# One wide matmul for the two parts of an operand, with a weight load and the first turn of a loop moved beside it

## What is computed

```python
h = rms_norm(x, g_mix)
q, k, v, cb, cc, cx, ga, gc = jnp.split(h @ w_in + b_in, pts, axis=-1)
q, k = apply_rope(q, positions), apply_rope(k, positions)
y_attn = sliding_window_attention(q, k, v, sinks) @ w_attn_o
y_conv = (cb * causal_short_conv(cc * cx, w_conv)) @ w_conv_o
merged = jax.nn.sigmoid(ga) * y_attn + jax.nn.sigmoid(gc) * y_conv
x = x + merged @ w_out
h = rms_norm(x, g_ffn)
x = x + moe_ffn(h, w_router, b_router, w_gate, b_gate, w_up, b_up, w_down, b_down)
return rms_norm(x, g_final)
```

## Time and profile before

| | us |
|---|---|
| median of 3 executions | 1192.78 |
| lowest, highest | 1192.71, 1193.74 |
| the profiled execution, its own time | 1192.05 |
| its span in the trace | 1190.2 |

### The profile page before, as it was taken

How to read it: one execution, slowest core, us unless ns; L and a number is a source line. 1 busy time by engine, 2 the same in 40 slices (tenths; PEclk the granted TensorE clock), 3 DMA queues, 4 the chain that set the end, 5 groups by cost and what they waited for, 6 DMA issues and landing times.

```text
span 1190.2 us, 18119 instructions
## 1 busy us (share of the span) xinstructions
PE 1119.3 (94%) x7454; PEld 572.4 (48%) x7454; DVE 364.4 (31%) x653; ACT 212.5 (18%) x393; POOL 128.2 (11%) x98
## 2 busy tenths in 40 slices
PE   8899999999999999999999999999999999999996
PEld 7899999984343333333333333333333333333342
DVE  6966785673111122111111111111111111111121
ACT  5566655451000000000000000000000000000001
POOL 4453444430000000000000000000000000000000
PEclk9999999999999999999999999999999999999999
DMA  8444666799999999999999999999999999999995
GB/s 283 143 154 157 220 201 217 245 399 413 427 428 426 428 428 428 428 428 428 428 428 428 428 428 427 428 426 428 428 428 428 430 428 428 429 429 428 427 426 218
DMA packets 71834, 448.06 MB, mean 376 GB/s; under 512 B 5497, under 2 KB 45781, under 8 KB 46709
## 3 DMA queue, kind: packets, MB, share of 16 engines
q1 hardware_dynamic: 71328, 446.75, 91.2%
q10 hardware_dynamic: 469, 0.77, 0.2%
HBM read 446.06 MB, written 1.05 MB: 376 GB/s over the span
## 4 chain that ended last, share of the span: by engine, by line
PE 48%; DMA 45%; DVE 3%; issue 2%; ACT 1%; SPq 0%; DVEq 0%; ACTq 0%
PE psum L686 26%; DMA ring<-in_w_up 23%; DMA ring<-in_w_gate 17%; PE psum L465 9%; PE psum L469 4%; DMA ring<-in_w_down 3%; PE psum L699 2%; PE psum L651 2%; DMA ring<-in_w_out 1%; PE psum L712 1%; DMA ring<-in_w_in 1%; ACT work L1016 1%; DVE w L1107 1%; PE psum L666 1%; PE psum L482 0%
## 5 line engine op out<-in xcount | busy, mean ns | idle before, releaser
L686 PE MATMUL psum<-ring,work 128*64 128x512 f32 x3072 | 686.3, 595 | 50.7 <-DMA ring<-in_w_gate 28.9
L686 PEld LDWEIGHTS psum<-ring,work 128*64 128x64 f32 x3072 | 212.4, 137 | 473.8 <-issue 363.1
L1343 DVE TENSOR_SCALAR work<-psum 128x512 f32<-128x512 f32 x32 | 22.1, 692 | 417.4 <-PE psum L686 417.4
L1476 POOL TENSOR_TENSOR w<-ring,w 128x1024 fp32r<-128x1024 f32 x38 | 100.7, 2657 | 108.0 <-ACT w L873 105.5
L1514 POOL COPY chosen<-pick 96x64 bf16 (+1 forms) x32 | 7.5, 234 | 868.8 <-PE psum L712 868.8
L465 PE MATMUL psum<-hL,w 128*128 128x256 f32 x384 | 95.3, 286 | 1.1 <-ACT w L873 0.6
L465 PE MATMUL psum<-hH,w 128*128 128x256 f32 x384 | 94.1, 283 | 0.0
L1107 DVE TENSOR_TENSOR w<-ring,w 128x1024 fp32r<-128x1024 f32 x38 | 80.1, 2112 | 37.7 <-ACT w L873 37.7
L1348 DVE TENSOR_SCALAR work<-psum 128x512 f32<-128x512 f32 x32 | 22.1, 692 | 192.8 <-PE psum L686 192.8
L873 ACT CAST w<-ring 128x1024 fp32r<-128x1024 f32 x74 | 74.4, 1048 | 27.8 <-PE psum L469 20.2
L465 PEld LDWEIGHTS psum<-hL,w 128*128 128x128 f32 x384 | 73.6, 192 | 4.0 <-issue 2.2
(11 more groups left out here) (202 smaller groups left out, 833.4 us busy)
## 6 DMA issues: line engine op xcount, KB each, us to landing
ring<-in_w_gate SPq DMA_DIRECT2D x64, 2048.0 KB, 38.1
ring<-in_w_up SPq DMA_DIRECT2D x63, 2048.0 KB, 39.7
ring<-in_w_down SPq DMA_DIRECT2D x61, 2048.0 KB, 39.3
ring<-in_w_in SPq DMA_DIRECT2D x26, 1024.0 KB, 5.0
ring<-in_w_down SPq DMA_DIRECT2D x6, 1024.0 KB, 37.6
ring<-in_w_conv_o SPq DMA_DIRECT2D x4, 1024.0 KB, 5.0
ring<-in_w_attn_o SPq DMA_DIRECT2D x4, 1024.0 KB, 5.2
ring<-in_w_out SPq DMA_DIRECT2D x4, 1024.0 KB, 6.2
```

What stands on the lines that cost most here:

```text
L686: mm = pe.matmul(psum[64 * h:64 * h + 64, b, :], src[:, k, :], w[:, k2, h * 512:(h + 1) * 512], start=(bias_of is None and k == 0), stop=( ...
L1343: v.tensor_scalar(gm, psum[:, 4, :], LIMIT, None, ALU.min).then_inc(gmin_ready, 1)
L1476: g.tensor_tensor(wL[:, par, 0, :, :], slot(s).rearrange("p (k n) -> p k n", k=KB)[:, :, 0:P], wH[:, par, 0, :, :].bitcast(F32), ALU.subtr ...
```

## The change

- Seven of the eight output-projection pieces go through a new function, `project_both`: zH and zL (and aH and aL) now lie side by side in one tensor, and one matmul with 512 columns multiplies wH with both. The high sum and the low sum land in two halves of a bank; each half m has a bank of its own, so pieces use pairs of banks. ScalarE copies the low sums to SBUF (`low_taken`), VectorE adds them to the high sums before it multiplies with the gate. The last a piece stays as it was.
- ScalarE's order in this stage: the split of the next piece before the cast of mH of the pair before.
- SyncE: the load into z's slot stands before the third `w_out` piece, the load into a's slot alone before the fourth.
- First turn: ScalarE's split of piece 3 stands ahead of the loop and of the copies of k; in the loop, `split_high_in_turn(i, 1)` at the start of a turn becomes `split_high_in_turn(i, 7)` at the end of the turn before it.
- One unused matmul before the ranks in place of two.

```diff
+PAIRS = ((4, 5), (0, 1), (2, 3))
...
-        zH, zL = parts("zH", at_slot(6), [P, KB, T]), parts("zL", at_slot(7), [P, KB, T])
-        aH, aL = parts("aH", at_slot(8), [P, KB, T]), parts("aL", at_slot(9), [P, KB, T])
+        zz, aa = parts("zz", at_slot(6), [P, 2, KB, T]), parts("aa", at_slot(8), [P, 2, KB, T])
+        zH, zL, aH, aL = zz[:, 0], zz[:, 1], aa[:, 0], aa[:, 1]
...
             for nth, src in enumerate(tail):
-                if n == NP1 - 1:
+                if n == NP1 - 2:
                     sp.wait_ge(blocks_done, 2 * (NIN + 2 * NKV - 1))
                     load_run(0, 2, 2)
+                if n == NP1 - 1:
                     sp.wait_ge(blocks_done, 2 * (NIN + 2 * NKV))
                     load_run(0, 3, 3)
...
+            def project_both(b, n, par, both, between=None):
+
+                for m in range(2):
+                    if m and between is not None:
+                        between()
+                    pe.wait_ge(wH_ready, n * 2 + (m + 1))
+                    for k in range(KB):
+                        pe.matmul(bank(b[m]).rearrange("p (x t) -> p x t", x=2), wH[:, par, m, k, :], both[:, :, k, :],
+                                  start=(k == 0), stop=(k == KB - 1))
+                    pe.wait_ge((wL0_ready, wL1_ready)[m], n + 1)
+                    for k in range(KB):
+                        mm = pe.matmul(bank(b[m], 0, T), wL[:, par, m, k, :], both[:, 0, k, :], start=False, stop=(k == KB - 1),
+                                       skip_group_check=True)
                     mm.then_inc(blocks_done, 1)
...
-                    project_T(n % 3, n, n % 2, src)
+                    if n < NIN + 2 * NKV - 1:
+                        project_both(PAIRS[n % 3], n, n % 2, src)
+                    else:
+                        project_T(PAIRS[n % 3][0], n, n % 2, (aH, aL))
...
-            for n in range(KEEP_WARM):
-                pe.matmul(bank(2), ident, cst[:, 0:512], start=True, stop=True)
+            pe.matmul(bank(2), ident, cst[:, 0:512], start=True, stop=True)
...
+            split_high(3, 0, 16 * 2, 1)
             act_e.wait_ge(kz_ready, 1)
             act_e.wait_ge(rotated, 1)
...
             with act_e.Fori(0, NKV) as i:
-                split_high_in_turn(i, 1)
                 act_e.wait_ge(blocks_done, i * 12 + 6)
                 act_e.wait_ge(rotated, i + 1)
...
                 act_e.wait_ge(u_ready, i + 1)
+                split_high_in_turn(i, 7)
+
+            def sum_high(i):
+
+                act_e.wait_ge(msum_ready, i + 1)
+                nc.scalar.copy(mH[:, 2 * i:2 * i + 2, :], raw).then_inc(mH_ready, 1)
...
-                if n + 1 < NP1:
+                if n > NIN:
                     split_high(n + 1, (n + 1) % RING1, 16 * ((n + 1) // RING1 + 1), (n + 1) % 2)
                 i, second = (n - NIN) // 2, (n - NIN) % 2
-                if second and i < NKV:
-                    act_e.wait_ge(msum_ready, i + 1)
-                    nc.scalar.copy(mH[:, 2 * i:2 * i + 2, :], raw).then_inc(mH_ready, 1)
+                if i and not second:
+                    sum_high(i - 1)
+                if not second:
+                    act_e.wait_ge(rotated, NKV + 1)
+                    if i:
+                        act_e.wait_ge(merged_ready, i)
+                if n < NIN + 2 * NKV - 1:
+                    for m in range(2):
+                        act_e.wait_ge(blocks_done, 2 * n + m + 1)
+                        nc.scalar.copy((raw, swp)[second][:, m, :], psum[:, PAIRS[n % 3][m], T:2 * T]).then_inc(low_taken, 1)
+            sum_high(NKV - 1)
...
-                    v.tensor_tensor(flat(tmp), psum[:, n % 3, :], flat(gate[:, 2 * i:2 * i + 2, :]), ALU.mult).then_inc(branch_read, 1)
+                    a, b = PAIRS[n % 3]
+                    if n < NIN + 2 * NKV - 1:
+                        dve.wait_ge(low_taken, 2 * (n - NIN + 1))
+                        steps.link(v.tensor_tensor(tmp, psum[:, a:b + 1, 0:T], tmp, ALU.add))
+                    summed = flat(tmp) if n < NIN + 2 * NKV - 1 else psum[:, a, :]
+                    v.tensor_tensor(flat(tmp), summed, flat(gate[:, 2 * i:2 * i + 2, :]), ALU.mult).then_inc(branch_read, 1)
```

## The result

The changed kernel takes 1207.17 us (median of 4 runs, 1205.63 to 1208.83), the kernel before 1193.03 beside it (1192.71 to 1193.74). The ratio is 1.0118, with a 95% interval from 1.0106 to 1.0130: slower by 14.1 us. The forecast was 1200.4 with a range to 1205.5, so the direction was right, the size was half of the truth, and the time lies outside the range.

A forecast was written before the change was run, and what follows sets the result against it. The expert weights' DMA stream was taken to set the end, TensorE to be the bound before its restart. Head loop +8.3, projections and z slot -2.4, clock +1.7 gave +7.6: 1200.4 us, range 1188.0 to 1205.5.

The forecast's parts named there:

- the chain of the stall: Head loop: late table load delays q, VectorE's split falls behind GpSimd's, TensorE waits 3.4 us more per turn; +8.3 in sum.
- L1107 wins the port: Rival, head loop: VectorE's split goes before GpSimd's, costing only 1.2 us per turn; 1190.0 us, chance 0.14.
- the rotation itself is blocked: Rival, head loop: L1097 starts behind GpSimd, a turn costs 3.8 to 5; 1206 or more, chance 0.06 with a longer load.
- The table load costs nothing: Rival, head loop: the sequencer runs the load before the wait is met, turns take 39.4 us; 1185.1 us, chance 0.12.
- I take one, as 2.2 us was harmless: Head loop: of the four new TensorE waits, one brings a clock fall; +1.7 us, bounds 0 to 6.8.
- the warming matmul at 0: Before the first expert: removing one warming matmul was taken as 0, with bounds from -0.8 to +1.7 us.
- The combined matmul: Output projections: a 512-column matmul takes 227 ns for two of 256 columns at 240 together; 1.5 us saved.
- The z slot: SyncE queue: the load waiting for z is issued at the last z piece's end, before the third w_out piece; 0.9 us gained.
- the end of the kernel is this restart plus a constant: Expert weight stream: its last hole, at 229 to 230 us, ends with a restart that sets the kernel's end.
- The drain: Head loop: a table load behind a wait might add a drain of up to 1.4 us per turn, 5.5 in all; 1206.

The follow-up runs named there:

- z_back: loop_back_warm2 with the z slot undone too: the load waiting for the last z piece stands behind the third w_out piece again; 1193.08 us, ratio 0.9994.
- loop_back_warm2: loop_back with the second warming matmul ahead of the ranks put back; 1191.56 us, ratio 0.9988.
- loop_back: Changed kernel with the head loop, and what runs ahead of it on ScalarE, as in the kernel before; 1192.94 us, ratio 0.9996.
- warm_two: Changed kernel with the second warming matmul put back, all else as changed; 1205.62 us, ratio 1.0100.
- loop_alone: Kernel before with only the changed kernel's order of ScalarE's splits in and ahead of the head loop; 1207.27 us, ratio 1.0118.

## Why the prediction was right, and where it failed

**Right: the chain of the stall.** The table load behind the wait, VectorE's split of c = 2 behind GpSimd's, no wait for the rotation, TensorE waiting four times for L1237: all in the trace, and the two experiments at the table load and at GpSimd's splits show that each link is needed. Taken without the clock the head loop is 177.7 - 6.8 = 170.9, 42.7 a turn, against the 42.8 of the forecast. The rivals *L1107 wins the port* and *the rotation itself is blocked* did not happen. *The table load costs nothing* would have given 1185.1: with the load out of the way it is 1187.1.

**Failed: the clock.** The step that failed is "I take one, as 2.2 us was harmless". The forecast weighed four waits of 3.4 us against a single one of 2.2 that had left the clock at 1.00, and took one fall in four. All four fell: 6.8 in place of 1.7, an error of 5.1. The head loop grew by 14.7 where 8.3 + 1.7 = 10.0 was forecast, so the clock is all that was missing there. The sum with four falls was written down (0 to 6.8), but the range was cut at two falls without a reason; and by its own terms (1192.78 + 9.9 - 0.9 + 3.4) it ends at 1205.2 and not at 1205.5. The ground was thin as well. In the kernel with the old head loop and the old z slot (z_back), the same wait for the rotation, 2.2 us long, was followed by a fall:

```profile
43.50:47.00 3.50, 3.50 (x19) 2.85 (x16) 3.50 (x3) 0.00 (x0) 2.27 (x2) 0.51 0.05 10
```

In the kernel before this stretch ran at 1.00, as it did in three other traces with the old head loop. So one execution with a wait and no fall was no proof that such a wait is harmless, and it said nothing of one that is half as long again.

**Failed: the warming matmul at 0.** Its bound of +1.7 was the nearer value: removing it cost 1.0 to 1.4 between loop_back_warm2 and loop_back, and 1.6, not clear of the spread, between warm_two and the changed kernel. The reasoning "where DMA has work queued" was at best half right: in the traces, 3.4 us of lost clock put off the load of the half slot by 1.7.

**Too good: the two gains.** The combined matmul was priced at 227 ns and measured 230, the seven pieces saved 1.2 of the 1.5. The Trainium skill (TensorE: Matmul & The Clock Gate, Back-to-back issue gap), by its formula for an isolated matmul, would have 216 ns, and a saving of 0.2 by its own two figures; the trace disagrees on both. The z slot gave nothing that could be told from zero where 0.9 was counted: the step that failed is "the end of the kernel is this restart plus a constant". The restart was the last total stop of the stream, and the earlier trace rows showed it, but not the last place at which it lost bytes: the ring waits once more, for the first expert. How much of the 1.2 from the projections reaches the end is open. z_back, which has it alone, is at 0.9994 with both 0 and 1.2 in its interval.

**The sum as measured.** Head loop +14.7 (clock +6.8, the rest +7.9, of which 0.9 is between executions), start-up -0.8, all behind it +1.7, together the 15.6 of the spans. Of the last term 0.6 lies ahead of the first expert, which starts 84.33 after the projections did, against 83.72 in the earlier trace rows (1.2 less for the pieces and 1.7 more for the clock would make 0.5):

```profile
285.68 6.87 PE psum L706 x32
```

The remaining 1.1 lies in the experts and has no cause here: from the start of the projections to the end of the span it took 1002.8 before and 1001.6 to 1004.9 in the others, not in the order of what was done to them.

**The drain.** The read of q starts 0.01 behind the end of the table load (118.78 + 1.28, 120.07), also where the load stands behind an open wait. The Trainium skill (ScalarE: Activation LUTs, What ACT_TABLE_LOAD costs) has some 1.4 us more for a drain; the trace doesn't agree, and that the 1206 worked out from it lies near the measured time is luck: what filled the gap was the clock.

## What to carry to other kernels

When an instruction at the head of a loop is moved, look at what was attached to it: the table load belongs to whichever activation comes first, and a tiny activation in a gap of the engine keeps it off the path. Price a new wait of TensorE of some 3 us at its length plus a fall of the clock for each time it occurs (twelve of twelve here), and trust a shorter wait without a fall only if several executions show it. A load that is issued sooner may gain nothing if the buffers behind it don't come free sooner too: compare the bytes moved up to the point at which the stream is steady, not the hole alone.

## What was not expected of the hardware

A fall of the clock isn't a fixed answer to a wait. The same wait of 2.2 us left it at 1.00 in four traces and at 0.51 for 3.5 us in a fifth, with the same instructions around it; the longer waits for the softmax (3.2 on average) were followed by a fall each of the twelve times in the changed kernel, loop_alone and warm_two. Ahead of the first expert it is the same: with two warming matmuls the clock fell in four traces, the kernel before among them, and stayed at 1.00 in four. And a fall can be free: in z_back it took the place of a wait of 1.5 for the softmax in the same turn, and the head loop took 164.1 there, 163.9 in loop_back_warm2 without a fall.

In the rows here GpSimd's splits and VectorE's instructions with operands in SBUF alone go strictly in turns, and who asks first decides. The Trainium skill (SBUF — State Buffer, SBUF: two separate sides) calls it an exclusive lock for a whole instruction, for the one who starts first; the trace agrees, with a mean of 3.4 for a split of 1.22 that stands behind one of GpSimd's of 2.4. Where both waited, the one whose turn had not just been was served, in every row shown.
